# Neighbourhood attention: bias and maximum in one VectorE pass per head, and the scaling of the exponentials split between GpSimd and ScalarE

## The reference

```python
bias = rpb.astype(jnp.float32)[:, dr[:, None, :], dc[None, :, :]]
s_band = jnp.einsum('brqhd,brkhd->bhrqk', qg, kg) * scale + bias[None]
s_band = jnp.where(in_win[None, None, None], s_band, -jnp.inf)
s_ctx = jnp.einsum('brqhd,bkhd->bhrqk', qg, k_ctx) * scale
p = jax.nn.softmax(jnp.concatenate([s_band, s_ctx], axis=-1), axis=-1)
o = (jnp.einsum('bhrqk,brkhd->brqhd', p[..., :n_band], vg)
     + jnp.einsum('bhrqk,bkhd->brqhd', p[..., n_band:], v_ctx))
```

## Time and profile before

| | us |
|---|---|
| median of 3 runs | 2921.0 (2916.03 to 2923.47) |
| profiled execution | 2921.84 |
| its span | 2920.0 |
| TensorE busy | 2825.4 (97%) |
| VectorE busy | 1726.2 (59%) |
| ScalarE busy | 1033.0 (35%) |
| GpSimd busy | 262.0 (9%) |

### The profile page before, as it was taken

How to read it: one execution, slowest core, us unless ns; L and a number is a source line. 1 busy time by engine, 2 the same in 40 slices (tenths; PEclk the granted TensorE clock), 3 DMA queues, 4 the chain that set the end, 5 groups by cost and what they waited for, 6 DMA issues and landing times. The chain is left out here.

```text
span 2920.0 us, 47186 instructions
## 1 busy us (share of the span) xinstructions
PE 2825.4 (97%) x19482; PEld 2680.7 (92%) x19482; DVE 1726.2 (59%) x2584; ACT 1033.0 (35%) x1689; POOL 262.0 (9%) x201
## 2 busy tenths in 40 slices
PE   8999999998899999999999999999979999999998
PEld 6999999986699999999999999999945698999998
DVE  5667666647666656667555536467768748432334
ACT  4211225426864111145211126643334436211124
POOL 0000003000020000011000002000048511000002
PEclk9999999999999999999999999999989999999999
DMA  6445443520045534444453334622211134322233
GB/s 238 143 153 179 154 152 131 161 81 9 28 139 153 160 122 147 158 132 134 153 159 122 116 102 136 177 91 77 76 61 33 58 102 128 111 85 68 73 100 124
DMA packets 102631, 345.21 MB, mean 118 GB/s; under 512 B 10769, under 2 KB 27537, under 8 KB 100881
## 3 DMA queue, kind: packets, MB, share of 16 engines
q1 hardware_dynamic: 96786, 333.15, 35.6%
q10 hardware_dynamic: 5632, 9.05, 0.9%
HBM read 331.54 MB, written 10.62 MB: 117 GB/s over the span
## 5 line engine op out<-in xcount | busy, mean ns | idle before, releaser
L1808 PE MATMUL P<-xh,wh 128*128 128x320 f32 x4016 | 1003.1, 312 | 10.2 <-DVE xl L1232 3.8
L1808 PE MATMUL P<-xl,wh 128*128 128x320 f32 x4016 | 992.5, 310 | 0.0
L1808 PE MATMUL P<-xh,wl 128*128 128x320 f32 x4016 | 992.4, 310 | 0.0
L790 ACT CAST wh<-raw 128x1024 fp32r<-128x1024 f32 (+1 forms) x421 | 471.9, 1121 | 990.9 <-PE P L1808 835.2
L1189 DVE TENSOR_TENSOR wl<-raw,wh 128x1024 fp32r<-128x1024 f32 (+1 forms) x421 | 552.5, 1313 | 289.7 <-ACT wh L790 289.5
L1808 PEld LDWEIGHTS P<-xh,wh 128*128 128x128 f32 x4016 | 691.7, 188 | 26.0 <-issue 12.5
L1808 PEld LDWEIGHTS P<-xl,wh 128*128 128x128 f32 x4016 | 691.8, 188 | 0.9
L1808 PEld LDWEIGHTS P<-xh,wl 128*128 128x128 f32 x4016 | 691.7, 188 | 0.0
L1808 PE MATMUL P<-hh,wh 128*128 128x320 f32 x1408 | 380.1, 310 | 0.0
L1808 PE MATMUL P<-hl,wh 128*128 128x320 f32 x1408 | 377.9, 309 | 0.0
L1808 PE MATMUL P<-hh,wl 128*128 128x320 f32 x1408 | 377.8, 309 | 0.0
(11 more groups left out here) (251 smaller groups left out, 2282.0 us busy)
## 6 DMA issues: line engine op xcount, KB each, us to landing
raw<-wgu_d SPq DMA_DIRECT2D x206, 512.0 KB, 3.7
mraw<-wmod_d SPq DMA_DIRECT2D x128, 512.0 KB, 3.6
raw<-wdB_d SPq DMA_DIRECT2D x64, 704.0 KB, 4.1
raw<-wdA_d SPq DMA_DIRECT2D x32, 704.0 KB, 5.3
raw<-ain_d SPq DMA_DIRECT2D x28, 512.0 KB, 3.5
raw<-sz_d SPq DMA_DIRECT2D x26, 512.0 KB, 3.8
raw<-sx_d SPq DMA_DIRECT2D x24, 512.0 KB, 3.5
raw<-aout_d SPq DMA_DIRECT2D x16, 512.0 KB, 3.5
```

The costliest lines, as they stand in the source:

```text
L790: nc.scalar.copy(wh[:, u.u % SPLITS, 0:n], raw[:, u.u % 2, 0:n]).then_inc(hi_done, 1)
L1808: ins = nc.tensor.matmul(P[:, u.banks[i], 0:C], w[:, u.u % SPLITS, k * 128:(k + 1) * 128], m[:, k, C * h:C * h + C], start=(k == 0 and w i ...
```

## The change

For an "nl" job the maximum is now taken within `bias`, one step earlier than before, in three parts. First VectorE takes the maximum of the 128 cached columns of each head. Then, for each head, one `tensor_tensor_reduce` adds the bias to the 256 neighbourhood columns in place and takes the maximum of the result, starting from the first maximum. Then both are negated, which signals `nm_done`. `front` does nothing for such a job.

The scaling of the exponentials of all jobs but the "gl" ones is divided: head 0's is done by GpSimd with a `tensor_scalar`, head 1's by ScalarE as before. The semaphore `pn_done` becomes one for each head; a group of transposes waits for those of the heads that it holds.

```diff
-        pn_done = sem("pn_done")
+        pn_done = [sem("pn_done0"), sem("pn_done1")]
...
+            def shares(job):
+
+                i, q = job.i, job.i % 4
+                p = pb[:, i % 2, 0, 0:job.n]
+                pool.wait_ge(rc_done, i - 15)
+                G.tensor_scalar(p, p, st[:, 3, q, 0:1], None, ALU.mult).then_inc(pn_done[0], 1)
...
+                if u.p.name == "ain" and u.u == u.p.u1 - 1:
+                    for job in jobs[GLOBALS:]:
+                        shares(job)
...
                 act.wait_ge(rc_done, i - 15)
-                for h in range(2):
-                    p = pb[:, i % 2, h, 0:job.n]
-                    nc.scalar.activation(p, p, ACT.Copy, scale=st[:, 3, q, h:h + 1]).then_inc(pn_done, 1)
+                p = pb[:, i % 2, 1, 0:job.n]
+                nc.scalar.activation(p, p, ACT.Copy, scale=st[:, 3, q, 1:2]).then_inc(pn_done[1], 1)
...
             def bias(job):
 
+                q = job.i % 4
+                mx, own = st[:, 0, q, :], st[:, 1, q, :]
                 dve.wait_ge(qk_done, job.i + 1)
                 w = (0, 1, 1, 2)[job.b]
+                me(V.reduce_max(own, score(job)[:, :, 2 * WIN:job.n], AXX))
                 dve.wait_ge(tb_in[job.t % 2], 16 * (job.t // 2 + 1))
                 table = tb[job.t % 2].rearrange("p (h w c) -> p h w c", h=2, w=3)[:, :, w, :]
-                me(V.tensor_tensor(score(job)[:, :, 0:2 * WIN], score(job)[:, :, 0:2 * WIN], table, ALU.add))
+                me.wait()
+                for h in range(2):
+                    near = score(job)[:, h, 0:2 * WIN]
+                    me(V.tensor_tensor_reduce(near, near, table[:, h, :], 1.0, own[:, h:h + 1], ALU.add, ALU.max, mx[:, h:h + 1]))
+                me.wait()
+                V.tensor_scalar(own, mx, -1.0, None, ALU.mult).then_inc(nm_done, 1)
 
             def front(job):
 
                 i, q = job.i, job.i % 4
                 mx, nm = st[:, 0, q, :], st[:, 1, q, :]
+                if job.kind == "nl":
+                    return
                 dve.wait_ge(qk_done, i + 1)
-                if job.kind == "nl":
-                    me.wait()
...
-                    pe.wait_ge(pn_done, 2 * i + group[-1][0] + 1)
+                    for h in sorted({h for h, _ in group}):
+                        pe.wait_ge(pn_done[h], i + 1)
```

More of the change, by code:

```diff
@@ L1333, in shares @@
                 rc = V.reciprocal(st[:, 3, q, :], st[:, 2, q, :])
-                if job.kind != "gl":
+                if job.kind == "gl":
+                    me(rc)
+                    me.wait()
+                else:
                     rc.then_inc(rc_done, 1)
                     return
-                me(rc)
-                me.wait()
                 for h in range(2):
                     p = pb[:, i % 2, h, 0:job.n]
-                    V.tensor_scalar(p, p, st[:, 3, q, h:h + 1], None, ALU.mult).then_inc(pn_done, 1)
+                    V.tensor_scalar(p, p, st[:, 3, q, h:h + 1], None, ALU.mult).then_inc(pn_done[h], 1)
             def take(job):
```

## The result

The changed kernel takes 2928.5 us (median of 20 runs, 2921.7 to 2936.0), the kernel before 2921.0 (20 runs, 2915.3 to 2923.5). The ratio is 1.0029, 95% interval 1.0023 to 1.0036: slower by 0.29%; the medians themselves lie 7.6 us (0.26%) apart. The forecast was 2924 with 2915 to 2933, within 0.3%.

The account below looks back on a forecast made before the run. In the attention stage ScalarE's queue was taken to set the pace, in a ring with VectorE and TensorE. The late reciprocal and GpSimd's scaling gave +2.6 us on the 2921.0 median, stated as 2924, range 2915 to 2933.

Parts of the forecast that it names:

- Step 1: ScalarE loses one share (scaling of one head) a job in the attention stage; at most 11.0 us to win.
- Step 2: VectorE's work per neighbourhood job: 1.68 us after against 1.86 before, with fused passes taken as 0.51 us each.
- Rival C: VectorE's fused pass is slow, 0.85 us each, adding 5.4 us for 2929; chance 0.11.
- Steps 3 and 4: VectorE's reciprocal comes 1.05 us later behind the fused block; the ring through VectorE, ScalarE and TensorE costs 1.9 us.
- step 4: Ring of waits through TensorE, VectorE and ScalarE: 6.01 us for two jobs against 5.77, 1.9 us in all.
- Step 5: GpSimd's scaling taken as 0.83 us; second ring 5.27 us plus that, 6.10 for two jobs, costing 2.6 us.
- rival B: GpSimd becomes the bound, its share as long as 1780 ns adds: 10.2 us more, 2931; chance 0.13.
- the rings: Two cycles of waits over two jobs, through ScalarE's share (6.01 us) or GpSimd's scaling (6.10), against 5.77 before.
- What would show it: Expected signs: ScalarE holes of some 0.5 us ahead of its share, attention stage 61 to 66 us, GpSimd's scaling about 0.83.
- Step 6: Context and neighbourhood-context jobs of 128 columns: between -2.8 and +2.8 us, taken as 0.
- Rival A: ScalarE alone sets the pace, reciprocal not late: 8.2 to 11.0 us go, 2910 to 2913; chance 0.16 including partial form.

Follow-up runs that it names:

- the fused half alone: Against the kernel before, only bias and maximum fused for "nl" jobs, ScalarE scaling both heads and GpSimd nothing: 2929.5 us, ratio 1.0032.
- GpSimd's short scaling: Changed kernel with GpSimd scaling only 128 of the 384 columns of head 0, the other 256 left unscaled: 2923.1 us, ratio 1.0008 to the kernel before.
- two other kernels: Kernel before with only bias and maximum fused, 2929.5 us; changed kernel with GpSimd's scaling cut to 128 columns, 2923.1 us.
- the kernel with two filling products: Changed kernel plus two constant TensorE products ahead of the wait for scaled exponentials in "nl" jobs: 2928.2 us, ratio 1.0020 to the kernel before.
- the early block: Changed kernel with the bias block of job i+1 ahead of the evacuation of job i-2 on VectorE: 2921.2 us, ratio 1.0002 to the kernel before.

## Why the prediction was right, and where it was not

The time lies in the range and the sign of the forecast's shift is right, but the shift is 7.6 us where I had 2.6, at the very edge of the 0.3% that I called no change. Part of the hit is luck: the profiled execution, 2924.59, lies on the forecast of 2924.4, but its stage is 9.6 us longer, and the scan, which the change does not touch, gave 5.3 of them back.

- **Step 1**, the most that can be won, 11.0 us: ScalarE's busy time fell by 8.1, and nothing of it reached the end.
- **Step 2**, the block: right in the sum, with terms that cancel. The two passes start 0.41 us apart where I had 0.51, as the read of 0.14 us lies under the next pass; but from the start of the first maximum to the first pass it is 0.56 us (759.46 to 760.02), 0.11 more than I had. The block is 1.63 us for 1.65. Rival C is out.
- **Steps 3 and 4**, the late reciprocal: shown, by the move of that instruction (10 us less in the median) and by the fused half alone (1.0032). The sum of step 4, 6.01 us for two jobs, is near the 6.17 that two neighbourhood jobs take in the mean in a full-clock tile with GpSimd's short scaling.
- **Step 5**, GpSimd: the term was mis-sized, 0.83 us forecast and 1.24 measured. Its rows were two-input operations, and this one-input form is slower a column than they are: (1242 - 602) / 256 = 2.5 ns. With 1.24 us the same formula gives a ring of 6.51 and 5.9 us in place of 2.6, which would have been 2927. The Trainium skill's "roughly line-rate" for one input (GPSIMD Engine Reference, Engine selection) is contradicted by this row: VectorE does the same scaling of 640 columns in 0.55 us (line 1341, "gl" jobs), under 0.9 ns a column. I gave rival B 0.13; its own test, over 0.5 us of wait a job, came out true for part of the jobs.
- **The clock** has no term in my sum, though the earlier trace rows showed a column for it. In the profiled execution the stage has 20.5 us more at half clock; at the 1.3 us for 3.4 that two other kernels show, this is an estimated 7.9 us of the 9.6, which leaves 1.7 for the rings. Against that, the formula with 1.24 us gives the rings 5.9 us, and the kernel with two filling products, which has as much half clock in the stage as before, has a stage 5.9 us longer than before, its filling included. So the rings' part lies between 1.7 and 5.9 us by these estimates. In the medians, the mean clock of 0.9879 instead of 0.990 at 2.1 us for each 0.001 is some 4.5 of the 7.6 us. These are extrapolations. The two causes are not independent either, as the half clock of the changed kernel comes where TensorE waits for the ring and mostly goes when that wait is filled or shortened. How much the changed kernel's rings would cost at a steady clock was not isolated; for the fused half alone it was, 1.4 us a tile.
- **What would show it**: holes ahead of ScalarE's share, yes (8.3 us); the stage of 61 to 66 us, no (70.4).
- **Step 6**, no cost in the jobs of 128 columns: right for jobs 17 to 20, which take 8.7 us before and after. **Rival A** falls: no kernel gains whose reciprocal stands behind the whole block.

## What to carry to other kernels

Before work is merged on an in-order engine, list what comes to stand behind it: here a merge that spared 0.2 us of work put a 0.16 us reciprocal a microsecond later, and that cost more than the 0.5 us a job that the rest of the change had freed; moving the reciprocal forward again repaired it without any change of the work. Where engines form a ring over two jobs, write the ring's sum, and look at the order first. Look at the clock of a stage in which TensorE has holes: the half clock that came with them here slowed the same ring once more.

## What the hardware showed that I had not expected

- A VectorE scaling of two columns from SBUF to SBUF is held up by a GpSimd scaling of 384 columns that runs: 0.45 us instead of 0.17, ending 0.02 to 0.03 us behind it, when it starts 0.81 us behind GpSimd's start; 0.34 us, ending 0.64 us ahead of GpSimd's end, when it starts 0.26 us behind. With its source in PSUM it takes 0.16 us at either place. The Trainium skill's page "SBUF — State Buffer", Who interferes with whom, describes such a lock between the two engines, held for the whole instruction; the first case agrees, the second does not, as the negation got through in the middle of GpSimd's. I had cited the page and looked at the long instructions alone, while a small one was hit. The reductions and evacuations, which read PSUM, kept their times beside GpSimd (0.95 and 0.29 us).
- In the changed kernel the half clock begins within a 1.00 us hole of TensorE and lasts 6.8 us, in each of the last three tiles at the same place; with the holes filled it vanishes from these tiles. With the early block a hole of the same length brought none.
- A fp32 product of 128 columns with constants shows as two instructions, 0.11 us apart in a run of them; five such products take 1.4 us, twice what I had counted.
